# One decoder layer on one core: half of the first modulation slabs multiplied unsplit, half of h made early, and the norms taken by halves of the tokens

## The reference, cut to what matters

```python
mod = silu(c) @ w_ada + b_ada                      # 6 x 1024: sh1, sc1, g1, sh2, sc2, g2
h = rmsnorm(x, norm_pre_mix) * (1 + sc1) + sh1
... # q, k, v, g, xr, gr from h @ w_in; retention, RG-LRU recurrence, two branches
mixed = (ga * branch_ret + gb * branch_rnn) @ w_out
x = x + g1 * rmsnorm(mixed, norm_post_mix)
h2 = rmsnorm(x, norm_pre_ffn) * (1 + sc2) + sh2
fg, fu = split(h2 @ w_ffn_in, 2)                   # 2816 channels each
x = x + g2 * rmsnorm((silu(fg) * fu) @ w_ffn_out, norm_post_ffn)
```

## Time and profile before

| | us |
|---|---|
| median of 3 runs (lowest, highest) | 1518.69 (1514.62, 1520.46) |
| the profiled execution: its time | 1519.44 |
| the profiled execution: span from first to last instruction | 1517.3 |
| PE busy (share of the span) | 1421.0 (94%) |
| DVE, ACT, POOL busy | 818.3, 565.6, 221.8 |
| bytes moved by DMA | 172.67 MB |

### The profile page before, as it was taken

The page is one execution under the profiler, slowest core; times in us unless marked ns, Lnnn a source line. Parts: engine busy times, 40 slices in busy tenths (PEclk is TensorE's granted clock), DMA queues, the critical chain, the costliest instruction groups (busy, mean ns, idle before and its releaser), DMA issues.

```text
span 1517.3 us, 23874 instructions
## 1 busy us (share of the span) xinstructions
PE 1421.0 (94%) x10168; PEld 1305.5 (86%) x10168; DVE 818.3 (54%) x1014; ACT 565.6 (37%) x751; POOL 221.8 (15%) x304
## 2 busy tenths in 40 slices
PE   5799999899999999999999999998599999999993
PEld 2499999778897698799879888997499999999993
DVE  4748888755435476348546744864733333332224
ACT  5467777444333232333233233333522222222220
POOL 2312322100013303302220330000200000000002
PEclk9899999999999899999999999999799999999997
DMA  8122222365634425523442452223032322222221
GB/s 324 70 85 70 70 84 85 108 220 198 205 105 136 147 71 167 166 91 115 164 139 77 146 174 98 85 95 130 1 98 84 97 85 84 90 87 78 88 77 59
DMA packets 48344, 172.67 MB, mean 114 GB/s; under 512 B 5360, under 2 KB 5488, under 8 KB 47856
## 3 DMA queue, kind: packets, MB, share of 16 engines
q1 hardware_dynamic: 37872, 135.51, 27.2%
q0 software_dynamic: 9216, 33.56, 6.8%
q10 hardware_dynamic: 1152, 2.10, 0.4%
HBM read 149.82 MB, written 21.32 MB: 113 GB/s over the span
## 4 chain that ended last, share of the span: by engine, by line
PE 65%; DVE 6%; ACT 1%; issue 1%; ACTq 0%; DVEq 0%
PE ps L658 55%; PE ps L867 2%; PE ps L878 2%; PE ps L850 1%; PE ps L894 1%; PE ps L904 1%; PE ps L896 1%; DVE mo L1655 1%; DVE x_res L1656 1%; DVE s_lo L1468 0%; PE ps L725 0%; PE ps L807 0%; DVE rsn L1651 0%; PE ps L820 0%; DVE work L1533 0%
## 5 line engine op out<-in xcount | busy, mean ns | idle before, releaser
L658 PE MATMUL ps<-h_hi,w_hi 128*128 128x272 f32 x2240 | 475.1, 294 | 26.7 <-DVE h_lo L1675 10.8
L658 PE MATMUL ps<-h_hi,w_lo 128*128 128x272 f32 x2240 | 466.8, 290 | 0.0
L658 PE MATMUL ps<-h_lo,w_hi 128*128 128x272 f32 x2240 | 466.0, 290 | 0.0
L658 PEld LDWEIGHTS ps<-h_hi,w_hi 128*128 128x128 f32 x2240 | 357.7, 190 | 33.9 <-issue 23.1
L1293 DVE TENSOR_TENSOR w_lo<-raw,w_hi 128x1024 fp32r<-128x1024 f32 (+2 forms) x196 | 236.2, 1207 | 277.6 <-ACT w_hi L996 274.0
L658 PEld LDWEIGHTS ps<-h_lo,w_hi 128*128 128x128 f32 x2240 | 356.3, 191 | 0.0
L658 PEld LDWEIGHTS ps<-h_hi,w_lo 128*128 128x128 f32 x2240 | 353.5, 191 | 0.0
L996 ACT ACTIVATE w_hi<-raw 128x1024 fp32r<-128x1024 f32 (+2 forms) x196 | 202.0, 1031 | 284.4 <-PE ps L658 229.3
L1568 DVE SCALAR_TENSOR_TENSOR state<-state,ps 128x512 f32<-128x512 f32 x64 | 41.1, 683 | 113.0 <-PE ps L904 112.9
L1811 POOL TENSOR_TENSOR mo<-mo,rsn 128x512 f32<-128x512 f32 x6 | 9.6, 1597 | 565.0 <-DVE rsn L1651 565.0
L658 PE MATMUL ps<-a_hi,w_hi 128*128 128x272 f32 x352 | 72.9, 288 | 2.1 <-DVE a_lo L1302 2.1
(11 more groups left out here) (224 smaller groups left out, 1901.6 us busy)
## 6 DMA issues: line engine op xcount, KB each, us to landing
raw<-in_w_head SPq DMA_DIRECT2D x48, 512.0 KB, 3.6
raw<-in_w_fin SPq DMA_DIRECT2D x44, 512.0 KB, 3.5
ada_late<-in_w_ada SPq DMA_DIRECT2D x32, 512.0 KB, 4.7
state<-in_state POOLq DMA_DIRECT2D x32, 512.0 KB, 4.2
out_rs<-state POOLq DMA_DIRECT2D x32, 512.0 KB, 3.5
raw<-in_w_rnn SPq DMA_DIRECT2D x24, 512.0 KB, 3.6
ada_raw<-in_w_ada SPq DMA_DIRECT2D x16, 512.0 KB, 14.3
raw<-in_w_bret SPq DMA_DIRECT2D x16, 512.0 KB, 3.5
```

The lines of the kernel that those rows point to most:

```text
L658: mm = nc.tensor.matmul(dst[:, half, :], a, b[:, half * HALF:(half + 1) * HALF], start=first and j == 0, stop=last and j == 2)
```

## The change

**First stage.** Of each chunk, slabs 0 and 2 are rounded and split as before; slabs 1 and 3 are multiplied as they are, in fp32, by `csil`. The chunks come in the order 0, 2, 1, 3. x is loaded in four parts, `con` first, and squared into eight places. POOL's multiplication by `rs_in` moves to DVE. When chunks 0 and 2 are turned, DVE and ACT make tiles 0 to 3 of h (`first_input(0)`, `hi_of_first(0)`); the last chunk is turned in the middle of PE's tile `xr` 0, and tiles 4 to 7 follow.

**Around wo.** `wo` 0 to 4 stay whole; 5, 6 and 7 are multiplied for the first 272 columns and then for the other 272 (`half_passes`). The norm, the sum, the second norm and the second h are made for each half. The first three pairs `fg`, `fu` are multiplied by halves too; their six slabs have places of their own (`early_hi`, `early_lo`, in memory that `a_hi` and `a_lo` take later) and stand between those of `wo`. `x_res` is loaded ahead of them. The second norm's scale and reciprocal are one DVE operation, the shift is in ACT's rounding. POOL has no part in the sums any more.

**End.** `fo` 7 is multiplied by halves, the norm, the sum and the stores of y go by halves (16 DMAs).

```diff
-START_SLABS = ADA_START * ADA_PARTS
+FIRST = (0, 2, 1, 3)
+FIRST_SPLIT = (0, 2)
...
+    for c in FIRST:
+        for i in FIRST_SPLIT:
+            chunk_slab(ADA_PARTS * c + i)
...
+    early = [(name, n) for n in range(EARLY) for name in ("fg", "fu")]
     for m in range(KD):
...
+        pl.add_slab(("wo", m, "w", 0), KD * P)
+        if m >= KD - len(early):
+            pl.add_slab((*early[m - KD + len(early)], "w", 0), KD * P)
...
+    held = held_halves()
+    for i in range(0, len(held), 2):
+        pl.add_halves(held[i:i + 2])
...
+    for half in range(2):
+        for n in range(EARLY):
+            pl.add_halves([("fg", n, half), ("fu", n, half)])
+            for name in ("fg", "fu"):
+                pl.step((name, n, "w", 0), (name, n, half))
...
+            sp.dma_start(con[:], w["con"]).then_inc(con_in, 16)
+            load_x(0)
...
-            sp.dma_start(x_in[:], w["x"]).then_inc(x_loaded, 16)
-            sp.dma_start(con[:], w["con"]).then_inc(con_in, 16)
-            load_to(START_SLABS + 1)
+            for i in range(1, 4):
+                load_x(i)
+            for c in FIRST:
+                for i in range(ADA_PARTS):
+                    n = first_place(c, i)
+                    sp.dma_start(ada_raw[:, n, :], w["w_ada"][c, i]).then_inc(ada_in[n], 16)
+            load_to(pl.slab[("gr", 0, "w", 0)])
...
-            load_to(pl.slab[("wo", KD - 1, "w", 0)])
+            load_to(pl.slab[("wo", KD - 2 * EARLY, "w", 0)])
             sp.wait_ge(mix_ready, KD)
+            states_stored(sp)
             sp.dma_start(xr_[:], w["x"]).then_inc(xres_in, 16)
             load_to(len(pl.slabs) - 1)
-            for k in NORM_ORDER:
...
+            for half in range(2):
+                for k in range(KD):
+                    sp.wait_ge(y_done, KD * half + k + 1)
+                    sp.dma_start(out["y"][:, k, cols_of(half)], xr_[:, k, cols_of(half)]).then_inc(stored, 16)
...
+                for j, (a, b) in enumerate(((whi, x_hi), (whi, x_lo), (wlo, x_hi))):
+                    mm = nc.tensor.matmul(dst, a, b[:, cols_of(half)], start=first and j == 0, stop=last and j == 2)
+                return mm
...
+                if c < ADA_START and i not in FIRST_SPLIT:
+                    n = first_place(c, i)
+                    pe.wait_ge(ada_in[n], 16)
+                    for j in range(2):
+                        mm = nc.tensor.matmul(dst[0:NSEQ, :], csil[:, 2 * i + j, :],
+                                              ada_raw[:, n, j * ADA_CHUNK:(j + 1) * ADA_CHUNK], start=False,
+                                              stop=i == ADA_PARTS - 1 and j == 1, skip_group_check=True)
+                    if i == ADA_PARTS - 1:
...
+                for k in ks:
+                    pe.wait_ge(xsq_ready, KD * half + k + 1)
+                    mm = nc.tensor.matmul(dst[:, 0:HALF], ccol("ones"), x1_sq[:, k, :], start=k == 0, stop=k == KD - 1)
...
+            def turn_first(n):
+                pe.wait_ge(row_ready, n + 1)
+                ada_turn(ada_row0[:, n % 2, :], ps[:, 4 + n // 2, 8 * NSEQ * (n % 2):], turned0)
+            for n, c in enumerate(FIRST):
+                for i in range(ADA_PARTS):
+                    modulation(ADA_PARTS * c + i)
+                if n:
+                    turn_first(n - 1)
...
+                project(("xr", n), [KD], h_hi, h_lo, h_ready if n == 0 else None, 0,
+                        before_tile=None if n else {KD // 2: lambda: turn_first(ADA_START - 1)})
...
-            for m in range(KD):
+            for m in range(KD - len(HELD)):
                 project(("wo", m), [KD], h_hi, h_lo, mix_ready if m == 0 else None, 0)
-            total(post, rsn, norm_summed, 1)
-            for k in range(KD):
-                add_squares(pre2, sqn[:, k % 2, :], k, KD, 2 * KD, sq_used)
-            for n in range(NF):
-                project(("fg", n), [KD], h_hi, h_lo, h_ready if n == 0 else None, KD)
...
+            for i, key in enumerate(held_halves()):
+                claim_half(key)
+                for k in range(KD):
+                    if i == len(HELD) and k == KD // 2:
+                        total_half("post", 0, 1)
+                    mm = half_step(key, k)
+                mm.then_inc(multiplied, 1)
+            add_squares(0, range(KD))
+            total_half("post", 1, 2)
+            for half in range(2):
+                for n in range(EARLY):
+                    both = [(name, n, half) for name in ("fg", "fu")]
+                    for key in both:
+                        claim_half(key)
+                    for k in range(KD):
+                        if (half, n, k) == (0, EARLY - 1, 0):
+                            add_squares(1, range(0, KD - 2))
+                        if (half, n, k) == (0, EARLY - 1, 3):
+                            add_squares(1, range(KD - 2, KD))
+                        if n == 0:
+                            pe.wait_ge(h_ready, KD * (1 + half) + k + 1)
+                        for key in both:
+                            mm = half_step(key, k)
+                            if k == KD - 1:
+                                mm.then_inc(multiplied, 1)
...
+            for half in range(2):
...
+                    for j in range(n):
+                        mm = half_passes(out_tile(last)[:, half, :], s, j * P, a_hi[:, k, :], a_lo[:, k, :], half, k == 0,
+                                         k == NF - 1)
+                        k += 1
+                    if half or i == len(FO_PARTS) - 1:
+                        mm.then_inc(multiplied, 1)
+                    if half and i == 0:
+                        total_half("post2", 0, 3)
+            total_half("post2", 1, 4)
...
+            square_input(0)
...
+            for n, c in enumerate(FIRST):
+                split_to(pl.slab[("ad", c, "w", FIRST_SPLIT[-1])] + AHEAD)
+                act.wait_ge(chunk_done, n + 1)
+                if n >= 2:
+                    act.wait_ge(turned0, n - 1)
+                do(A(ada_row0[:, n % 2, :], ps[0:2 * NSEQ, c, :], ACT.Copy), row_ready, wait=False)
+                if n == 2:
+                    hi_of_first(0)
+            hi_of_first(1)
...
+            def square_of_sum(half, k):
+                act.wait_ge(x1_ready, KD * half + k + 1)
+                do(A(x1_sq[:, k, :], xr_[:, k, cols_of(half)], ACT.Square), xsq_ready, wait=False)
...
+            def hi_of_second(half, k):
+                act.wait_ge(h_scaled, KD * half + k + 1)
+                do(A(h_hi[:, k, prompt_of(half)], mo[:, k, prompt_of(half)], ACT.Identity, bias=mod[:, 3 * KD + k, 0:1]),
+                   h_hi_ready, wait=False)
...
-            std([("post", 0), ("post", 1)], rsn, D, eps_rms)
-            for i, k in enumerate(NORM_ORDER):
-                act.wait_ge(x1_ready, k + 1 if k < DVE_TILES else 1)
-                if k >= DVE_TILES:
-                    act.wait_ge(x1_pool, k - DVE_TILES + 1)
-                if i >= 2:
-                    act.wait_ge(sq_used, KD + i - 1)
-                do(A(sqn[:, i % 2, :], xr_[:, k, :], ACT.Square), sq_ready, wait=False)
-            std([("pre2", 0), ("pre2", 1)], rsn, D, eps_rms)
-            hi_of_second()
-            for n in range(NF):
+            for m in range(KD - len(HELD)):
...
+            split_to(pl.slab[("wo", KD - 1, "w", 0)])
+            for m in HELD:
+                held_tile(m, 0)
+            std(("post",), 0, rsn, D, eps_rms)
+            split_to(pl.slab[("fu", EARLY - 1, "w", 0)])
+            x1 = iter(range(KD))
+            for m, n in zip(HELD, (2, 3, 3)):
+                held_tile(m, 1)
+                for _ in range(n):
+                    square_of_sum(0, next(x1))
+            std(("pre2",), 0, rsn, D, eps_rms)
+            std(("post",), 1, rsn, D, eps_rms)
+            for k in range(KD):
+                hi_of_second(0, k)
+            silu_half(0, 0)
+            for k in range(KD):
+                square_of_sum(1, k)
+            std(("pre2",), 1, rsn, D, eps_rms)
+            silu_half(1, 0)
+            for k in range(KD):
+                hi_of_second(1, k)
+            silu_half(2, 0)
+            ahead(("fg", EARLY))
...
+            ahead(("fo", KD - 1), 2)
+            for half in range(2):
+                gated_half("fo", KD - 1, half, out_tile(("fo", KD - 1))[:, half, :], gate2, KD + KD - 3,
+                           took(("fo", KD - 1)) if half else (mo_ready, 2))
+                std(("post2",), half, rsn, D, eps_rms)
...
+            split_to(pl.slab[("ad", FIRST[1], "w", FIRST_SPLIT[-1])])
             dve.wait_ge(std_ready, 1)
-            do(V.reciprocal(rs_in[:], rs_in[:]), rs_ready, wait=False)
-            for c in range(1, ADA_START):
-                split_to(pl.slab[("ad", c, "w", ADA_PARTS - 1)] + AHEAD)
+            do(V.reciprocal(rs_in[:], rs_in[:]))
+            for k in range(KD):
+                if k == KD // 2:
+                    split_to(pl.slab[("ad", FIRST[2], "w", FIRST_SPLIT[-1])])
```

(103 more changed lines are left out.)

356 lines of the change are left out of this document (192 added, 164 removed).

## The result

The changed kernel takes **1481.28 us** (median of 4 runs, 1479.25 to 1481.9) where the kernel before takes 1519.15 beside it (1514.62 to 1520.46): ratio 0.9754, 95% interval 0.9731 to 0.9776. That is 37.9 us less; the forecast was 1486, from a sum of 32.2 us.

The account below looks back on a forecast made before the run. PE, busy 94% of the span, was taken as the bound, so only its stretches without a tile could be won. Gains of 9.3, 15.9 and 7.0 sum to 32.2 us: 1519.4 becomes 1487.2, forecast 1486 by the median, range 1478 to 1498.

Parts of the forecast that it names:

- part 1: First stage: unsplit slabs, reordered work and early tiles of h bring the eighth tile at 58.0 instead of 67.3; 9.3 us gained.
- part 2: Around `wo`: halves let PE start `fg` 0 earlier, while DVE works on the second half; 15.9 us gained.
- part 3: The end: `fo` 7 by halves, with POOL's share and its slowing of DVE gone; 7.0 us gained.
- `rg_w` and `xr` 1 keep their 10.5 us: First stage: the time from `rg_w` to the start of `xr` 1 stays as before (67.3 to 77.83).
- upper bound (12): First stage: 12 us gained if the gap before `xr` 1 shrinks to 2 us and the slow stretch behind it goes.
- The 0.5 charged for the load of `x_res`: In `wo`: with `x_res` ahead of its last five slabs, `wo` 3 may come late; 0.5 us lost, between 0 and 3.
- The 14.6 us: Around `wo`: the gain if every table switch also costs a 1.38 us drain, making `product_half(1, 0)` 1.3 us later.
- U+25.5: End of the span, 25.5 us after the first half of `fo` 7 is done; forecast at 1510.3.
- (1): Early `fg`, `fu` pairs: low clock holds through their first halves; 8.4 us less gain, 1495 us, chance 0.13.
- (2): First stage: low clock holds through the modulation; the stage loses 6 us, total 1501.5, chance 0.08.
- (3): `half_passes`: weight loads no longer lie under matmuls, 564 cost 0.065 us more each; 37 us, total 1523, chance 0.03.
- (4): Around `wo`: slabs come late behind `x_res`, so PE stands between tiles, two waits of 5 us; 1496 us, chance 0.04.

Follow-up runs that it names:

- the repetition: The changed kernel run once more with nothing changed: 1482.67 us, ratio 0.9762 to the kernel before.
- first profile: The changed kernel's own first profiled execution, with a span of 1479.1 us, beside its median of 1481.28 us.
- The last experiment: The kernel before with one line moved, so that the slab of `xr` 1 loads ahead of `rg_w`: 1512.7 us, ratio 0.9958.
- the earlier turn: The changed kernel with the last chunk turned ahead of `xr` 0 instead of in its middle: 1477.21 us, ratio 0.9725.

## Why the prediction was right, point by point

The mechanism stood in all three parts; the sum was 6.0 us short of the 38.2 between the first pair of spans and 2.5 short of the 34.7 that the repetition gives. The term that was mis-sized most is in the first stage. Gains in us, each read between the same places of the traces:

| term | forecast | first profile | repetition |
|---|---|---|---|
| part 1, to the start of `bn` | 9.3 | 12.9 | 11.0 |
| part 2, from the start of `wo` to the start of `fo` | 15.9 | 16.6 | 16.0 |
| part 3, from the start of `fo` 7 to the end | 7.0 | 7.4 | 7.6 |
| the clock in `bn` to `wo` and in `fo` | none | 1.3 | 0.1 |
| all | 32.2 | 38.2 | 34.7 |

- **Part 1.** Nearly every step came out: PE's sums ended at 16.9 (forecast 18), DVE was through with its eight lo's at 35.2 (36), `xr` 0 started at 44.34 (44.7), `rg_w` at 56.84 (58.0), `xr` 1 at 67.53 (68.5). One of these hits has luck in it: an unsplit slab took PE 1.81 us (17.77 to 19.58) and not 1.6, but PE began 1.1 us earlier, and DVE had its eighth lo only at 35.2 in any case. Of the 3.6 us that were missing, 1.0 is the earlier `xr` 1: the first four k of `xr` 0 began at the full clock and took 4.5 us, not the 5.4 put in. The other 2.6 are the step that failed, "`rg_w` and `xr` 1 keep their 10.5 us", by what it left out. The slab does come 10.7 us behind `rg_w`, so the start of `xr` 1 is as the step has it. But PE, whose `xr` 0 ran mostly at the low level, was at work until 65.4 and stands only 2.10 us ahead of `xr` 1, not 3.42, and the low stretch behind it stays away. The forecast had this as its upper bound (12) and took the other end. The last experiment shows on the old kernel that stretch and gap go together. It isn't sure at 2 us: the repetition had a gap of 2.62 us there and a low stretch again behind it, and with it the part gave 11.0.
- **Part 2.** The second halves of `wo` start at T = 1029.10; `fg` 0 started at T+20.0 (forecast 20.1), the second half at T+47.7 (48.2). A tile of h took 0.95 us and not 0.87: the fused operation of DVE takes 0.50 for 272 columns, and 0.44 had been put in. Against that PE was slow for 3.4 us behind the first stop and not 5.9; as it was slow for twice as long there in the repetition, that is the execution's luck and not the kernel's. The 0.5 charged for the load of `x_res` ahead of the last slabs met its number for another reason. `wo` took 0.9 us longer than before, but only 0.2 of it was lost ahead of `wo` 3; 0.5 went to the total of the first half, which stands among the second halves (1030.47 to 1031.18 for two steps of 0.127), and 0.2 to the pace of the halves, 0.127 us a matmul where the whole tiles have 0.125.
- **The table loads.** 1069.76 to 1071.06 is 1.30 us for a load of 1.28: the silu starts right behind it, as the root did in the earlier trace rows. The drain of 1.38 us that the Trainium skill ("ScalarE: Activation LUTs", What ACT_TABLE_LOAD costs) adds to every switch is not in this trace either: ACT's root ahead of the load ends at 1069.75, so no time is left on either side of it. The 14.6 us that the part would give by it are 1.4 to 2.0 too low.
- **Part 3.** Behind the last matmul 8.0 us were gained, and `fo` 7 itself took 0.5 longer (17.2 for 16.7): from its start to the end of the span 40.84 us became 33.39. U+25.5 was forecast, U+25.0 measured with U at 1454.05, the start of the second half. The experiment with `fo` 7 whole puts nearly all of it down to the halves of the tile; that POOL's share went, which the forecast named beside it, is worth at most some 0.5 together with the halves of the norm.
- The lower end of the range doesn't follow from its own terms: the three upper bounds 12, 19 and 8 give 39 us, which is 1479.7 from the median shown, and 1478 was written.

The rivals. (1) The low clock through the first halves: it lasted 3.4 us, to 1052.9, and twice that in the repetition, of 18 us of halves. (2) The low clock through the modulation: PE ended it at 41.5, and from 15 to 45 us the granted clock was 1.00. (3) Weight loads uncovered: `half_passes` goes at 0.127 us a matmul (1028.34 to 1029.10 for six), nearly the pace of the whole tiles. (4) Late slabs at `wo`: the longest wait of PE in it is 0.3 us, where the sum had put two of 5. All four were ruled out by the first profile. That a low stretch behind a stop on the path costs time was right; that one behind a stop of another place costs the same was not asked, and the run with matmuls of constants shows that it doesn't.

## What to carry to other kernels

Halving a tile pays where another engine then works beside PE, and by somewhat less than PE multiplies in that time (6.9 us for 8.3 at the end, 13.4 for 18 around `wo`); the smaller pieces by themselves gave 0.5 and 3.2. When an early piece is made so that PE may start, look at what PE's own queue puts behind it for the second piece: a turn of 0.4 us behind four k of a tile cost as much as the whole early half had given. And read what a queue has ahead of a small, urgent load: one line that moved a slab past 1.5 MB was worth 2.4 us on top of the earlier turn (1477.21 to 1474.84), 2.3 or 3.7 by itself, depending on which median of the changed kernel it is held against, and 6.6 in the kernel before.
